# Gated feed-forward: the first two weight slots of each gate/up pair by seven block products instead of eight

## What is computed

```python
h2 = rmsnorm(x, g_ffn)
gu = h2 @ w_gu                                              # w_gu is 2048 x 11264
x = x + (jax.nn.silu(gu[..., :D_FF_2]) * gu[..., D_FF_2:]) @ w_down   # D_FF_2 = 5632
```

## Time and profile before

| | before |
|---|---|
| median of 3 runs | 2481.94 us |
| span of the profiled execution (first to last instruction) | 2480.3 us |
| that execution's own time | not recorded apart; the runs lie 1.6 us above the span |
| TensorE busy | 2474.2 us, 100% |
| VectorE busy | 1482.4 us, 60% |
| ScalarE busy | 1386.7 us, 56% |
| GpSimd busy | 67.0 us, 3% |
| DMA | 208 GB/s mean |

### The profile page before, as it was taken

The page is one execution under the profiler, slowest core; times in us unless marked ns, Lnnn a source line. Parts: engine busy times, 40 slices in busy tenths (PEclk is TensorE's granted clock), DMA queues, the critical chain, the costliest instruction groups (busy, mean ns, idle before and its releaser), DMA issues.

```text
span 2480.3 us, 28682 instructions
## 1 busy us (share of the span) xinstructions
PE 2474.2 (100%) x11017; PEld 2050.3 (83%) x11017; DVE 1482.4 (60%) x1607; ACT 1386.7 (56%) x1695; POOL 67.0 (3%) x78
## 2 busy tenths in 40 slices
PE   9999999999999999999999999999999999999999
PEld 8888888888888888888888888888888888888887
DVE  5888576556555465676577645556555545555554
ACT  6886565446455455556676645546654444544443
POOL 0110000000000000011100000000000000000000
PEclk9999999999999999999999999999999999999999
DMA  8997668677677676577756666667777666766665
GB/s 284 263 265 205 204 194 222 211 207 230 195 212 211 191 217 195 170 210 215 230 179 202 197 196 202 200 193 208 219 208 204 203 194 200 209 203 195 203 196 170
DMA packets 348553, 515.34 MB, mean 208 GB/s; under 512 B 113840, under 2 KB 114152, under 8 KB 348168
## 3 DMA queue, kind: packets, MB, share of 16 engines
q1 hardware_dynamic: 343592, 496.63, 67.1%
q0 software_dynamic: 4688, 16.93, 3.1%
q10 hardware_dynamic: 144, 0.01, 0.0%
HBM read 476.52 MB, written 4.47 MB: 194 GB/s over the span
## 4 chain that ended last, share of the span: by engine, by line
PE 98%; DVE 1%; ACT 0%; issue 0%; DMA 0%; POOL 0%; SPq 0%; DVEq 0%; ACTq 0%; POOLq 0%
PE acc L467 32%; PE acc L469 32%; PE acc L468 32%; PE tp L503 0%; PE acc L512 0%; PE po L684 0%; PE sc L660 0%; DMA planesT_mix<-planes_mix 0%; ACT yb L943 0%; PE acc L484 0%; PE acc L483 0%; PE acc L482 0%; PE po L686 0%; DVE h L1500 0%; ACT w_hi L757 0%
## 5 line engine op out<-in xcount | busy, mean ns | idle before, releaser
L1201 DVE TENSOR_TENSOR w_lo<-raw,w_hi 128x1024 fp32r<-128x1024 f32 x888 | 1078.3, 1224 | 846.0 <-ACT w_hi L757 845.1
L757 ACT ACTIVATE w_hi<-raw 128x1024 fp32r<-128x1024 f32 x888 | 934.3, 1060 | 988.0 <-PE acc L469 974.3
L467 PE MATMUL acc<-w_lo,a_hi 128*128 128x512 f32 x2304 | 899.7, 391 | 0.7 <-issue 0.7
L469 PE MATMUL acc<-w_hi,a_lo 128*128 128x512 f32 x2304 | 896.7, 389 | 0.0
L468 PE MATMUL acc<-w_hi,a_hi 128*128 128x512 f32 x2304 | 896.4, 389 | 0.0
L469 PEld LDWEIGHTS acc<-w_hi,a_lo 128*128 128x128 f32 x2304 | 432.5, 188 | 90.3
L467 PEld LDWEIGHTS acc<-w_lo,a_hi 128*128 128x128 f32 x2304 | 432.6, 188 | 90.1 <-issue 1.7
L468 PEld LDWEIGHTS acc<-w_hi,a_hi 128*128 128x128 f32 x2304 | 432.7, 188 | 89.0
L467 PE MATMUL acc<-w_lo,b_hi 128*128 128x512 f32 x1104 | 430.0, 389 | 0.3 <-DVE w_lo L1201 0.3
L469 PE MATMUL acc<-w_hi,b_lo 128*128 128x512 f32 x1104 | 429.5, 389 | 0.0
L468 PE MATMUL acc<-w_hi,b_hi 128*128 128x512 f32 x1104 | 429.5, 389 | 0.0
(11 more groups left out here) (197 smaller groups left out, 982.8 us busy)
## 6 DMA issues: line engine op xcount, KB each, us to landing
raw<-w_in_dram SPq DMA_DIRECT2D x272, 512.0 KB, 4.5
raw<-w_down_dram SPq DMA_DIRECT2D x216, 512.0 KB, 4.0
raw<-w_gu_dram SPq DMA_DIRECT2D x176, 512.0 KB, 4.1
raw<-w_up_dram SPq DMA_DIRECT2D x128, 512.0 KB, 3.9
raw<-w_out_dram SPq DMA_DIRECT2D x64, 512.0 KB, 4.4
raw<-w_branch_dram SPq DMA_DIRECT2D x32, 512.0 KB, 4.1
tap_sum<-tap_add POOLq DMA_DIRECT2D x20, 512.0 KB, 7.1
skew_dram<-line_dram POOLq DMA_DIRECT2D x12, 192.0 KB, 4.6
```

The source lines that it names most:

```text
L467: nc.tensor.matmul(out, xh, wl, start=s == 0 and k == 0, stop=False)
L469: mm = nc.tensor.matmul(out, xl, wh, start=False, stop=s == n - 1 and k == KS - 1)
L757: nc.scalar.activation(w_hi[:, ring], raw[:, ring], ACT.Copy).then_inc(hi_ready, 1)
L1201: nc.vector.tensor_tensor(w_lo[:, ring], raw[:, ring], w_hi[:, ring].bitcast(F32), ALU.subtract).then_inc(lo_ready, 1)
```

## The change

In ten of the eleven pairs (all but the very first) the first two slots of the gate unit and the first two of the up unit are taken together. They form a 2 x 2 arrangement of blocks (two depths of 256 rows by gate and up columns), the 256 tokens give two token tiles, and the eight block products of such a 2 x 2 by 2 x 2 product are replaced by seven, by Strassen's identity in Winograd's form. Each of the seven is 2 k tiles x 3 = 6 matmuls. Of the seven weight operands three are the blocks themselves and four are sums of blocks; the four sums are made in place in `quad_raw`, a buffer of four blocks, by GpSimd. The activation operands of the sums (`x_hi`, `x_lo`) are made once, in the first pair. Each of the seven weight operands goes through the ring of 4 as a slot did: rounded by ScalarE, split by VectorE. The products go partly to `acc`, partly to the four other PSUM banks (`tp`, `sc`, `po`), from which VectorE combines them into `parts_ff`; the combination is added when VectorE evacuates the units. Silu now runs from SBUF on ScalarE, and the scale of the up unit is applied in the product `zz`.

The core of the diff (the rest is numbering, the same loops re-indexed, and the combination of the parts):

```diff
+def feed_forward_slots():        # 7 quad uses, then the 12 plain slots of a pair
...
+            quad = (b, j) != (0, 0)
+            if quad:
+                kind += [(f, None) for f in range(QUAD)]
+            n = 2 * (SPU - Q0 if quad else SPU)
+            kind += [(None, r + i) for i in range(n)]
...
+        quad_raw = at("quad_raw", 156, [P, 2, 2, KS, W])
...
@@ SyncE
+            def load_quad(p, i):
+                b, j = (p // 4, p % 4)
+                if i == 0:
+                    if quad_of(p):
+                        sp.wait_ge(lo_ready, FF_PAIR[p - 1][0] + QUAD)
+                    else:
+                        sp.wait_ge(slot_used, G_FF)
+                sp.dma_start(quad_raw[:, i // 2, i % 2], gate_up(b, j, i % 2, i // 2)
+                             ).then_inc(quad_in[i], 16)
...
@@ TensorE
+            def quad_product(g, f, out, xh, xl, start, stop=False):
+                pe.wait_ge(lo_ready, g + f + 1)
+                ring = (g + f) % RING
+                for k in range(KS):
+                    wh, wl = w_hi[:, ring, k, :], w_lo[:, ring, k, :]
+                    nc.tensor.matmul(out, xh[:, k], wl, start=start and k == 0, stop=False)
+                    nc.tensor.matmul(out, xh[:, k], wh, start=False, stop=False)
+                    mm = nc.tensor.matmul(out, xl[:, k], wh, start=False, stop=stop and k == KS - 1)
+                mm.then_inc(slot_used, 1)
...
+                quad_product(g, 0, tp[:, 0, :], *tile_of(0, 0), True, True)
+                pe.wait_ge(evacuated, u - 1)
+                quad_product(g, 1, acc[:, 0, 0, :], *tile_of(1, 0), True)
+                quad_product(g, 2, po[:, :], x_hi[:, 0], x_lo[:, 0], True, True)
+                quad_product(g, 3, sc[:, :], x_hi[:, 1], x_lo[:, 1], True, True)
+                quad_product(g, 4, tp[:, 1, :], x_hi[:, 2], x_lo[:, 2], True, True)
+                quad_product(g, 5, acc[:, 0, 1, :], *tile_of(1, 1), True)
+                pe.wait_ge(evacuated, u)
+                quad_product(g, 6, acc[:, 1, 0, :], x_hi[:, 3], x_lo[:, 3], True)
...
@@ ScalarE
+                    i, need = ((0, None), (2, None), (0, 1), (1, 2), (0, 3), (2, 4), (3, None))[f]
+                    if need is None:
+                        act.wait_ge(quad_in[i], 16 * (q + 1))
+                    else:
+                        act.wait_ge(quad_sum, 4 * q + need)
+                    src = quad_raw[:, i // 2, i % 2]
+                act.wait_ge(slot_used, g - RING + 1)
+                nc.scalar.activation(w_hi[:, g % RING], src, ACT.Copy).then_inc(hi_ready, 1)
...
+                    nc.scalar.activation(parts_ff[:, 0], tp[:, 0, :], ACT.Copy).then_inc(lead_out, 1)
...
+                    for tk in range(TT):
+                        a_ = nc.scalar.activation(ev[:, 0, tk], ev[:, 0, tk], ACT.Silu,
+                                                  scale=rs[:, 5, tk:tk + 1])
...
@@ VectorE (use is the split of one slot or one quad block)
+            def up_out(j):
+                g, _, _ = FF_PAIR[pair_of(b, j)]
+                dve.wait_ge(slot_used, g + QUAD + 2 * (SPU - Q0))
+                nc.vector.tensor_tensor(ev[:, 1], acc[:, 1], parts_ff[:, 1::2], ALU.subtract
+                                        ).then_inc(evacuated, 1)
...
+                    if j and (b, j) != (0, 1):
+                        up_out(j - 1)
+                    uses(g + 4, g + 8)
+                    if j:
+                        gated_product(j - 1)
+                    uses(g + 8, g + 9)
+                    if j:
+                        part_planes("ff", zz, (z_ready, z + j))
...
@@ GpSimd
+            def quad_add(to, one, other):
+                nc.gpsimd.tensor_tensor(quad_raw[:, to // 2, to % 2], quad_raw[:, one // 2, one % 2],
+                                        quad_raw[:, other // 2, other % 2], ALU.add
+                                        ).then_inc(quad_sum, 1)
+            for p in range(1, len(FF_PAIR)):
+                g, q = FF_PAIR[p][0], quad_of(p)
+                pool.wait_ge(quad_in[0], 16 * (q + 1))
+                pool.wait_ge(quad_in[1], 16 * (q + 1))
+                pool.wait_ge(lo_ready, g + 1)
+                quad_add(0, 0, 1)
+                pool.wait_ge(quad_in[3], 16 * (q + 1))
+                pool.wait_ge(quad_sum, 4 * q + 1)
+                quad_add(1, 1, 3)
+                pool.wait_ge(lo_ready, g + 3)
+                pool.wait_ge(quad_sum, 4 * q + 2)
+                quad_add(0, 0, 3)
+                pool.wait_ge(quad_in[2], 16 * (q + 1))
+                pool.wait_ge(quad_sum, 4 * q + 3)
+                quad_add(2, 2, 0)
```

More of the change, by code:

```diff
@@ L420, in _, with load_ff @@
[L420 to L430, removed]
+            def load_ff(r, src):
+                sp.wait_ge(lo_ready, FF_USE[r - RING] + 1)
+                sp.dma_start(raw[:, r % RING], src).then_inc(landed[r % RING], 16)
@@ new lines, in ff_block @@
+            def ff_block(b):
+                pairs, down_slots = FF_PAIRS[b], FF_SLOTS[b]
+                u = U_FF + b * (3 * NCH)
+                z, sp_ = 32 + b * NCH, S_FF + b * (2 * NCH)
+                for j in range(pairs):
+                    p = pair_of(b, j)
+                    g, _, quad = FF_PAIR[p]
+                    if quad:
+                        quad_slots(p, u + 2 * j)
+                        after_quad(g + QUAD, 0)
+                        after_quad(g + QUAD + SPU - Q0, 1)
+                        continue
+                    slots(g, u, 0, SPU, a_hi, a_lo, split0=S_N3)
+                    slots(g + SPU, u + 1, 0, SPU, a_hi, a_lo, pair=1)
+                gd, ud = FF_DOWN[b][0], u + 2 * pairs
@@ L744, in _ @@
+            for b in range(3):
+                ff_block(b)
         @block.scalar
@@ L1753, in _, with use @@
                 part_planes("mix", h[:, :, j], (h_ready, 2 * NCH + j + 1))
-            def ff_block(g, u, b, pairs, down_slots, last):
+            def use(g):
+                f, r = FF_KIND[g - G_FF]
+                if f is None:
+                    src = raw[:, r % RING]
+                else:
+                    q = quad_of(max(p for p in range(len(FF_PAIR)) if FF_PAIR[p][0] <= g))
+                    i = (0, 2, 0, 1, 0, 2, 3)[f]
+                    src = quad_raw[:, i // 2, i % 2]
+                dve.wait_ge(hi_ready, g + 1)
+                nc.vector.tensor_tensor(w_lo[:, g % RING], src, w_hi[:, g % RING].bitcast(F32),
+                                        ALU.subtract).then_inc(lo_ready, 1)
@@ new lines, in uses, with x_values @@
+            def uses(g_from, g_to):
+                for g in range(g_from, min(g_to, G_FF + len(FF_KIND))):
+                    use(g)
+            def x_values():
+                dve.wait_ge(split_hi, S_N3 + 2)
+                dve.wait_ge(split_lo, S_N3 + 2)
+                nc.vector.tensor_tensor(x_val[:, :, :], a_hi[:, 0:2 * KS, :].bitcast(F32),
+                                        a_lo[:, 0:2 * KS, :].bitcast(F32), ALU.add
+                                        ).then_inc(x_form, 1)
@@ L1764, in ff_block @@
                         split_joined(S_N3 + 6, "mix", a_hi, a_lo, 12, G_FFN2)
[L1765 to L1768 removed]
+                        uses(g + RING + 3, g + RING + SPU)
                         mean_square(5, 46)
[L1770 to L1772 removed]
@@ L1784, in ff_block @@
+                    if j:
+                        lo_of(j - 1)
+                    uses(g + 18, g + 19 + RING)
+                up_out(pairs - 1)
+                gated_product(pairs - 1)
+                if last:
+                    split(S_FF + b * (2 * NCH) + 2 * (pairs - 1), b_hi, b_lo, 4 * (pairs - 1))
+                else:
+                    part_planes("ff", zz, (z_ready, z + pairs))
+                gd, ud = FF_DOWN[b][0], u + 2 * pairs
                 if b == 0:
```

319 lines of the change are left out of this document (233 added, 86 removed).

## The result

The changed kernel takes 2533.7 us (median of 4 runs, 2527.3 to 2534.4), the kernel before 2481.9 in the same job: a ratio on record of 1.0203, 95% interval 1.0190 to 1.0216 (the medians by themselves give 1.0209). It is slower, by 51.8 us, and lies above the range of the prediction, which ended at 2514; whether it is slower by more than 2% the interval leaves open. The profiled execution is the fastest of the four: 2527.3 us, span 2525.5, 45.2 us above the span before.

The account below looks back on a forecast made before the run. TensorE, busy for the whole span, bounds the kernel. From 2481.9 us, 13.6 saved on matmuls against waits of 10 x 2.85 + 2 x 1.2 = 30.9 gave +17.3, forecast 2499 us; range 2467.5 to 2514.

Parts of the forecast that it names:

- splits and additions exclude each other: VectorE's splits and GpSimd's additions take turns, standing in one line before operand 4; forecast case 2499 us, chance 0.56.
- Rival 1: No exclusion between VectorE's splits and GpSimd's additions: nothing waits, 2468.3 us; chance 0.22.
- rival 2: Exclusion with GpSimd additions at their lower bound of 1.76 us: wait 1.1 us per pair, 2481.7 us; chance 0.06.
- A: Length of one GpSimd addition of 1024 elements: taken as 2.2 us, between 1.76 and 2.64.
- The price of nothing for combinations, evacuations and `zz`: VectorE's added work behind the seven products: about 23 us in 12 slots of 32.6 us, so hidden at no cost.
- the 13.6 us for 60 matmuls: TensorE saving in ten pairs, eight block products becoming seven: 60 x 0.2267 = 13.6 us, all on the path.
- `wide += ev`: VectorE instruction with two SBUF inputs, before split 4 in first pairs of blocks 1 and 2: 1.2 us more each.
- line in front of operand 4: Four additions and the splits, each waiting for the one before, delay the fifth product: 30.9 us of TensorE waits in all.
- The clock: TensorE's granted clock, 1.00 before; if it fell below 1.00 around the waits, the price would be higher; no size given.
- The loads: Block loads issued at least six slots, 16 us, before use against 4.1 us to land; no cost counted.
- Rival 4: Block loads arrive late through SyncE's queue, some 4 us a pair: 2508 us; chance 0.02.
- 4A - 5.95: TensorE's wait per pair before the fifth product, in us, from the addition length A: 2.85 us at A = 2.2.

Follow-up runs that it names:

- the run between them: Block loads moved to the end in the first pair only, against the changed kernel: 2524.82 us, ratio 1.0173 to the kernel before.
- the interleaved kernel with GpSimd's sums: Changed kernel with a plain gate slot after each product but the last and block loads at the pair's end: 2472.35 us, ratio 0.9962 to the kernel before.

## Why the prediction was right or wrong

**Direction and mechanism were right, the size was not.** It is slower because splits and additions exclude each other. That was read from one row, in one direction; the runs show both: a split in front of the third addition holds it up 1.1 us, an addition in front of split 4 makes it 2.44 us. They also show what no row of before could: fills, which only write, leave splits at 1.22 us. The Trainium skill, SBUF — State Buffer, section "Who interferes with whom", says the same, that the exclusion takes a GpSimd instruction that reads; the traces agree, with 1.224 us beside fills and up to 3.3 us beside additions. Rival 1 is out, and so is rival 2, since A is 2.34.

**The place was right**: ten waits, each before product 4, ended by VectorE's split (and two small ones before product 2, 1.2 us, not forecast), and none in the plain slots of the ten pairs that the combinations could have caused. The price of nothing for combinations, evacuations and `zz` held (additions of 8 elements: no idle time in the ten pairs). So did the 13.6 us for 60 matmuls: 13.7 with the products spread and the sums on VectorE. First pairs of blocks 1 and 2 were to wait 1.2 us more, for `wide += ev`; with loads out of the way they wait 0.8 and 1.1 more.

**Three terms were mis-sized.** The profiled execution, term by term; a pause costs TensorE some 0.16 us beyond the idle time, since a matmul's row is 0.39 us long and the next may start after 0.2267:

| term | forecast | measured | from |
|---|---|---|---|
| 60 matmuls | -13.6 | -13.6 | count |
| line in front of operand 4 | 30.9 | 33.7 | 32.1 idle with loads at the end, and 10 x 0.16 |
| block loads | 0 | 8.5 | 37.6 - 32.1; 3.0 in the first pair |
| slow clock | 0 | 17.1 | sum of (1 - clock) x time |
| sum | +17.3 | +45.7 | spans differ by 45.2 |

Of the 17.1 us some 1.1 lie inside pauses, where a slow clock costs nothing; with them left out the sum is 44.6.

1. *The clock.* The prediction named it ("If the clock falls below 1.00 around the waits, the price is higher than the sum") and gave it neither a term nor a rival. That is the failed step, put at nothing and measured at 17.1 us in the profiled execution: every row shown of before had TensorE at work and the clock at 1.00, so no row priced it, but a cost that nothing bounds belongs in the range. In the medians matmuls that fill the pause give back 13.4 and 11.9 us. The 13.4 are less than the 17.1, since these matmuls are not free: 170 of them are 38.5 us, and 5.6 us of idle time remain, against 37.6 us of idle time before.
2. *The loads.* This is the second failed step, also put at nothing. "With at least six slots, 16 us, until use, against 4.1 us to land" asks whether the block loads are late for their own use. They never are. What they do is stand in front of others: SyncE's wait on `slot_used` and four 512 KB transfers come ahead of the transposes of the planes (7.84 us for 2.64) and of ring loads (ScalarE waits 24 times). Rival 4 had this mechanism only as block loads missing their own date, and gave it 0.02. Measured, the loads are 8.5 us of idle time, with the slow stretches that follow 18 us of medians.
3. *A.* 2.34 us and not 2.2, within its bounds of 1.76 and 2.64. With 4A - 5.95 that alone is 0.56 us a pair; the pairs that no load disturbs stand still 3.1 us, 0.25 more than the 2.85 of the forecast, as the rest of the line came out 0.3 us shorter than I put it. That these two errors offset in part is luck.

Neither of the first two alone made the miss. With the pauses filled the kernel takes 2520.4, with the loads at the end 2515.8, and both lie above 2514. Without clock and loads the sum would have come close: forecast 2499, and the kernel with loads at the end and the pauses filled takes 2504.0, of which 14 matmuls a pair cover a pause of 3.1 us.

**Where 51.8 us went**, in medians: 2468.2 is the saving with nothing lost; +7.8 for products that stand together (2476.0); +28.0 for additions on GpSimd (2504.0); +11.9 for slow stretches (2515.8); +17.9 for the place of the block loads, slow stretches included (2533.7). The parts hold in this order of steps; the 28.0 contain the longer addition as well as the exclusion.

**Open**: why the clock falls after one pause of 2.97 us and not after the next. Also how the 17.9 us of the loads divide between the first pair and the others: the run between them moved half of it, and the clock scatters by some 4 us. And what the interleaved kernel with GpSimd's sums pays its 4.2 us for: its waits for splits add up to some 2.

## What to carry to other kernels

When work goes to GpSimd, write it in one line with VectorE's instructions that read two SBUF tiles, and ask how short the steps of TensorE are that this line must feed: the same forty additions cost 4 us between long slots and 28 between short ones (40 with the slow clock that followed), and VectorE itself, with no more work than it had room for, did the sums for nothing. A pause of TensorE of about 3 us is to be priced with the half-speed stretch that may follow it. A load that is early for its own use still stands ahead of something: look at what is behind it in its queue.

## What the runs showed that I had not expected

- Pauses of 2.97 and 2.98 us, with the same rows around them, were followed by 3.4 us at 1.2 GHz in three cases of seven. Over all the profiled executions the shortest pause with a fall was 2.38 us (additions of 768 elements), and the longest without one 3.47 us (loads at the end). After nine pauses of 0.56 us (sums on VectorE) no fall was seen; useless matmuls in the pause kept the clock at 1.00 in all twenty pairs where they were tried.
- GpSimd's addition of fp32 tiles in SBUF costs 0.20 us for 8 elements a partition (0.33 in the mean, with the six that waited for a split), 1.80 for 768 and 2.34 for 1024 at the shortest, so 2.1 ns an element; its memset of 1024 elements takes 0.95 us.
- Two DMA transposes behind a burst of 512 KB loads took 7.84 us to issue instead of 2.64; at five later places they took 5.2 to 5.7 us, where before the change the like took 2.6 to 3.4.
